# Modulation weights of a three-branch layer stack: from split products to 4-byte products in four column strips

## The reference, cut to what matters

```python
s_lat = jax.nn.silu(c)
s_ctx = jax.nn.silu(c_ctx)[None, :]
...
sh1, sc1, g1, sh2, sc2, g2 = jnp.split(s_lat @ ada_w[i] + ada_b[i], 6, axis=-1)
csh1, csc1, cg1, csh2, csc2, cg2 = jnp.split(s_ctx @ ada_w[i] + ada_b[i], 6, axis=-1)
```

## Time and profile before

| | |
|---|---|
| median of 3 runs | 2079.94 us (2079.64 to 2085.49) |
| profiled execution: time, span | 2084.67 us, 2082.9 us |
| mean granted TensorE clock | 0.943 |
| TensorE busy | 1849.3 us (89%), 12954 products |
| VectorE, ScalarE, GpSimd busy | 908.4, 959.8, 1317.7 us |
| chunks fetched, chunks split | 448, 447 |
| chain that ended last | issue 32%, TensorE 32%, GpSimd 31% |
| waits of TensorE for GpSimd | 46.3 us, all at modulation products (L774) |

### The profile page before, as it was taken

How to read it: one execution, slowest core, us unless ns; L and a number is a source line. 1 busy time by engine, 2 the same in 40 slices (tenths; PEclk the granted TensorE clock), 3 DMA queues, 4 the chain that set the end, 5 groups by cost and what they waited for, 6 DMA issues and landing times.

```text
span 2082.9 us, 36490 instructions
## 1 busy us (share of the span) xinstructions
PE 1849.3 (89%) x12954; PEld 1706.7 (82%) x12954; DVE 908.4 (44%) x1959; ACT 959.8 (46%) x1399; POOL 1317.7 (63%) x451
## 2 busy tenths in 40 slices
PE   5868998999978777999999965699999988888997
PEld 5867898999978776899999953588888877678997
DVE  3688544323335686554313368321221256443223
ACT  5623546544565434555545653532232343255443
POOL 6754578988886744598989961644444433136885
PEclk9988999999999989999999976899999989898999
DMA  6433355655654523465656651433232323114553
GB/s 216 164 127 103 112 176 187 209 196 190 203 184 147 177 91 101 144 210 190 209 186 205 203 188 51 139 101 98 92 101 89 101 76 101 38 64 140 178 189 109
DMA packets 67873, 301.31 MB, mean 145 GB/s; under 512 B 7424, under 2 KB 9728, under 8 KB 67584
## 3 DMA queue, kind: packets, MB, share of 16 engines
q1 hardware_dynamic: 66240, 296.69, 43.0%
q10 hardware_dynamic: 1472, 2.43, 0.3%
HBM read 298.04 MB, written 1.05 MB: 144 GB/s over the span
## 4 chain that ended last, share of the span: by engine, by line
issue 32%; PE 32%; POOL 31%; DVE 2%; ACT 1%; DVEq 1%; POOLq 1%; ACTq 0%
POOL wlo L728 31%; PE bank L762 10%; PE bank L766 10%; PE bank L765 10%; PE bank L1069 0%; DVE bank L1986 0%; PE bank L1073 0%; PE bank L1072 0%; PE bank L1108 0%; POOLq L732 0%; DVE split_acts L1519 0%; DVEq L2145 0%; PE bank L1096 0%; ACT bank L1391 0%; PE bank L1088 0%
## 5 line engine op out<-in xcount | busy, mean ns | idle before, releaser
L728 POOL TENSOR_TENSOR wlo<-raw,whi 128x1280 fp32r<-128x1280 f32 x447 | 1317.5, 2964 | 745.6 <-ACT whi L1142 743.9
L762 PE MATMUL bank<-split_acts,whi 128*128 128x256 f32 (+1 forms) x3556 | 1096.0, 308 | 86.9 <-DVE split_acts L1519 50.9
L765 PE MATMUL bank<-split_acts,whi 128*128 128x256 f32 (+1 forms) x3556 | 1081.4, 304 | 0.0
L766 PE MATMUL bank<-split_acts,wlo 128*128 128x256 f32 (+1 forms) x3556 | 1080.5, 304 | 0.0
L762 PEld LDWEIGHTS bank<-split_acts,whi 128*128 128x128 f32 x3556 | 693.6, 195 | 131.2 <-issue 58.5
L1142 ACT ACTIVATE whi<-raw 128x1280 fp32r<-128x1280 f32 x447 | 562.7, 1267 | 402.8 <-PE bank L762 347.0
L765 PEld LDWEIGHTS bank<-split_acts,whi 128*128 128x128 f32 x3556 | 694.7, 195 | 23.0 <-issue 0.2
L766 PEld LDWEIGHTS bank<-split_acts,wlo 128*128 128x128 f32 x3556 | 693.7, 195 | 23.2
L2018 DVE SCALAR_TENSOR_TENSOR acts<-bank,acts 128x256 f32<-128x256 f32 x120 | 54.1, 480 | 223.2 <-PE bank L766 223.2
L774 PE MATMUL bank<-whi,split_acts 128*128 128x256 f32 x384 | 107.8, 313 | 48.6 <-POOL wlo L728 46.3
L2032 DVE TENSOR_SCALAR acts<-bank 128x512 f32<-128x512 f32 (+1 forms) x64 | 35.7, 558 | 203.1 <-PE bank L766 203.1
(11 more groups left out here) (222 smaller groups left out, 1588.3 us busy)
## 6 DMA issues: line engine op xcount, KB each, us to landing
raw<-in_stream SPq DMA_DIRECT2D x448, 640.0 KB, 3.9
acts<-in_x SPq DMA_DIRECT2D x1, 1024.0 KB, 6.6
acts<-in_ctx ACTq DMA_DIRECT2D x1, 1024.0 KB, 6.6
out<-acts SPq DMA_DIRECT2D x8, 128.0 KB, 2.0
acts<-in_const ACTq DMA_DIRECT2D x1, 832.0 KB, 10.0
acts<-in_const SPq DMA_DIRECT2D x1, 772.0 KB, 9.2
acts<-in_p ACTq DMA_DIRECT2D x2, 256.0 KB, 4.2
acts<-in_par SPq DMA_DIRECT2D x1, 86.0 KB, 3.5
```

What stands on the lines that cost most here:

```text
L728: nc.gpsimd.tensor_tensor(wlo[slot][:, :], raw[slot][:, :], whi[slot][:, :].bitcast(F32), ALU.subtract).then_inc(lo_ready, 1)
L762: first = nc.tensor.matmul(out_ap, w_hi, hi_act(k), start=(k == 0), stop=False)
L765: nc.tensor.matmul(out_ap, w_hi, lo_act(k), start=False, stop=False)
L766: last = nc.tensor.matmul(out_ap, w_lo, hi_act(k), start=False, stop=(k == k_tiles - 1))
```

## The change

The weights of the modulation tiles are no longer split. A tile has two chunks of its own in the stream (eight atoms each, of ten that are fetched), and TensorE reads them straight from the raw buffer, with a stationary operand in 4-byte floats: 32 columns of a small `silu_c` that now lies among the 4-byte buffers. A chunk holds four of the eight parts of the contraction; part k of the first chunk goes to strip k of the array's columns and to partitions 32k to 32k+31 of the bank, the second chunk adds to the same strips. VectorE copies all 128 rows, and `turn_rows` contracts over 128 rows with a `pair` matrix of ones in rows 0 and 1 of every 32, which adds the four strips. The drain behind a tile stands where a count at the last product stood.

SP waits for a raw buffer by the kind of the chunk that was in it: `lo_ready` for a split chunk, `ada_used` (counted by TensorE) for an unsplit one. `chunk_plan` gives the order of both kinds; `keep_ahead` now counts raw chunks of both kinds, `RAW_AT[t] + 3`. A layer has 160 chunks, 124 split and 36 not; the second block 148, 124 and 24; in all 468 fetches and 372 splits. The order of a layer, A for an unsplit chunk, a point for a split one:

```diff
@@ -67,7 +67,7 @@
-            "wo": 8, "hg": 8, "hu": 8, "dn": 11, "pg": 8, "pp": 2, "ada": 16, "turn": 0}
+            "wo": 8, "hg": 8, "hu": 8, "dn": 11, "pg": 8, "pp": 2, "ada": 0, "turn": 0}
@@ -146,11 +146,30 @@
-LAYER_CHUNKS = -(-LAYER_ATOMS // (CHUNK_ATOMS * RING)) * RING
-def last_chunk(span):
-    return max(span[1] - 1, 0) // CHUNK_ATOMS
+SPLIT_CHUNKS = -(-LAYER_ATOMS // (CHUNK_ATOMS * RING)) * RING
+ADA_CHUNKS = 2
+ADA_ATOMS = 2 * KT // ADA_CHUNKS
+def chunk_plan(tiles, spans, split_chunks):
+    order, at, splits, adas = [], {}, 0, 0
+    for t in tiles:
+        if t[0] == "ada":
+            order += [("ada", adas + i) for i in range(ADA_CHUNKS)]
+            adas += ADA_CHUNKS
+        while splits * CHUNK_ATOMS < spans.get(t, (0, 0))[1]:
+            order.append(("split", splits))
+            splits += 1
+        at[t] = len(order) - 1
+    return order + [("split", n) for n in range(splits, split_chunks)], at
+ORDER, RAW_AT = chunk_plan(TILES, ATOM_SPAN, SPLIT_CHUNKS)
+RAW_OF = {c: i for i, c in enumerate(ORDER)}
+LAYER_CHUNKS = len(ORDER)
+LAYER_ADA_CHUNKS = LAYER_CHUNKS - SPLIT_CHUNKS
+assert LAYER_CHUNKS % RING == 0
@@ -159,10 +178,8 @@
-B2_ATOMS_ADA = (ADA_TILES - DEPTH * LAYER_ADA) * 2 * KT
-B2_ATOMS = B2_ATOMS_ADA + 16 + 4 * MLP_T * KT + 64 + 32 + 32 + 64
-B2_CHUNKS = -(-B2_ATOMS // (CHUNK_ATOMS * RING)) * RING
-N_CHUNKS = DEPTH * LAYER_CHUNKS + B2_CHUNKS
+B2_ATOMS = 16 + 4 * MLP_T * KT + 64 + 32 + 32 + 64
+B2_SPLITS = -(-B2_ATOMS // CHUNK_ATOMS)
@@ -208,7 +225,15 @@
+ORDER2, RAW_AT2 = chunk_plan(TILES2, ATOM_SPAN2, B2_SPLITS)
+RAW_OF2 = {c: i for i, c in enumerate(ORDER2)}
...
+FIRST_SPLIT2 = DEPTH * SPLIT_CHUNKS
+FIRST_ADA2 = DEPTH * LAYER_ADA_CHUNKS
+N_CHUNKS = FIRST_CHUNK2 + len(ORDER2)
+EARLY = sum(i < AHEAD for c, i in RAW_OF.items() if c[0] == "split")
+assert EARLY == sum(i < AHEAD for c, i in RAW_OF2.items() if c[0] == "split") == 0
+assert all(RAW_OF[("ada", i)] == RAW_OF2[("ada", i)] == i for i in range(RING))
@@ -300,9 +325,10 @@
-def modulation_atoms(a, n):
+def modulation_atoms(a, m):
+    n, part = divmod(m, ADA_CHUNKS)
...
-    return wide_columns(a["ada_w_2"][layer][:, n * 256:(n + 1) * 256], KT, 256)
+    return wide_columns(a["ada_w_2"][layer][:, n * 256:(n + 1) * 256], KT, 256)[part * ADA_ATOMS:(part + 1) * ADA_ATOMS]
@@ -503,6 +528,7 @@
+        silu_c = keep(2 * KT + 30)
@@ -707,12 +733,24 @@
-            with sp.Fori(1, N_CHUNKS // RING) as r:
-                for slot in range(RING):
-                    sp.wait_ge(lo_ready, r * RING + (slot - RING + 1))
-                    sp.dma_start(raw[slot][:, :], stream[bass.ds(r * RING + slot, 1)].rearrange("a p n -> (a p) n"))\
-                        .then_inc(raw_in[slot], 16)
+            def raw_free(order, c, splits_before, adas_before):
+                kind, n = order[c]
+                if kind == "split":
+                    sp.wait_ge(lo_ready, splits_before + (n + 1))
+                else:
+                    sp.wait_ge(ada_used, adas_before + (n + 1))
+            with sp.Fori(0, DEPTH) as lay:
+                for c in range(LAYER_CHUNKS):
+                    raw_free(ORDER, c, lay * SPLIT_CHUNKS, lay * LAYER_ADA_CHUNKS)
+                    sp.dma_start(raw[c % RING][:, :],
+                                 stream[bass.ds(lay * LAYER_CHUNKS + (c + RING), 1)].rearrange("a p n -> (a p) n"))\
+                        .then_inc(raw_in[c % RING], 16)
+            for c in range(len(ORDER2) - RING):
+                raw_free(ORDER2, c, FIRST_SPLIT2, FIRST_ADA2)
+                fetch(c % RING, FIRST_CHUNK2 + c + RING)
@@ -722,18 +760,18 @@
-            def lo_parts(slot, chunk):
-                pool.wait_ge(hi_ready, chunk + 1)
-                nc.gpsimd.tensor_tensor(wlo[slot][:, :], raw[slot][:, :], whi[slot][:, :].bitcast(F32),
+            def lo_parts(order, n, hi_count):
+                slot, source = n % RING, order[("split", n)] % RING
+                pool.wait_ge(hi_ready, hi_count)
+                nc.gpsimd.tensor_tensor(wlo[slot][:, :], raw[source][:, :], whi[slot][:, :].bitcast(F32),
...
-            used = DEPTH * LAYER_CHUNKS + -(-B2_ATOMS // CHUNK_ATOMS)
-            with pool.Fori(0, used // RING) as r:
-                for slot in range(RING):
-                    lo_parts(slot, r * RING + slot)
-            for slot in range(used % RING):
-                lo_parts(slot, used - used % RING + slot)
+            with pool.Fori(0, DEPTH) as lay:
+                for n in range(SPLIT_CHUNKS):
+                    lo_parts(RAW_OF, n, lay * SPLIT_CHUNKS + (n + 1))
+            for n in range(B2_SPLITS):
+                lo_parts(RAW_OF2, n, FIRST_SPLIT2 + n + 1)
@@ -766,20 +805,23 @@
-            def modulation(b, lay, base):
-                for k in range(KT):
-                    w_hi, w_lo, opens = weights(lay, base, 2)
-                    s4 = silu_c[:, k * P:(k + 1) * P]
-                    first = nc.tensor.matmul(b[:, 0:256], s4, w_hi, start=(k == 0), stop=False)
-                    if opens:
-                        first.then_inc(slots_used, 1)
-                    last = nc.tensor.matmul(b[:, 0:256], s4, w_lo, start=False, stop=(k == KT - 1))
+            def modulation(b, order, chunks_before):
+                for part in range(ADA_CHUNKS):
+                    c = order[("ada", Cursor.ada)]
+                    Cursor.ada += 1
+                    pe.wait_ge(raw_in[c % RING], chunks_before * (16 // RING) + (c // RING + 1) * 16)
+                    for strip in range(4):
+                        k = part * 4 + strip
+                        last = nc.tensor.matmul(b[32 * strip:32 * strip + 32, 0:256], silu_c[:, 2 * k:2 * k + 32],
+                                                raw[c % RING][:, strip * 256:(strip + 1) * 256],
+                                                start=(part == 0), stop=(part == ADA_CHUNKS - 1))
+                    last.then_inc(ada_used, 1)
...
-                    last = nc.tensor.matmul(b[:, 2 * i:2 * i + 2], rows[0:4, i * P:(i + 1) * P], C("pair")[0:4, :],
+                    last = nc.tensor.matmul(b[:, 2 * i:2 * i + 2], rows[:, i * P:(i + 1) * P], C("pair"),
@@ -789,10 +831,10 @@
-                Cursor.atom = 0
+                Cursor.atom = Cursor.ada = 0
...
-                    return lay * LAYER_CHUNKS + chunk
+                    return lay * SPLIT_CHUNKS + chunk
@@ -824,7 +866,8 @@
-                        modulation(b, lay, base).then_inc(gemm_done, 1)
+                        modulation(b, RAW_OF, lay * LAYER_CHUNKS)
+                        pe.drain().then_inc(gemm_done, 1)
@@ -1006,7 +1049,8 @@
-                    last = modulation(b, 0, base2)
+                    modulation(b, RAW_OF2, FIRST_CHUNK2)
+                    last = pe.drain()
@@ -1133,18 +1177,11 @@
-            def split(lay, base, chunk):
-                g = base(lay, chunk)
-                act.wait_ge(slots_used, g + 1)
-                act.wait_ge(raw_in[chunk % RING], (base(lay, chunk - chunk % RING) // RING) * 16 + 16
-                            if isinstance(g, int) else lay * (LAYER_CHUNKS // RING * 16) + (chunk // RING + 1) * 16)
-                sc.activation(whi[chunk % RING][:, :], raw[chunk % RING][:, :], ACT.Copy).then_inc(hi_ready, 1)
-            def ahead(lay, base, chunk):
-                while Split.chunk <= chunk + AHEAD:
-                    split(lay, base, Split.chunk)
-                    Split.chunk += 1
+            def split(n, source, splits_before, chunks_before):
+                act.wait_ge(slots_used, splits_before + (n + 1))
+                act.wait_ge(raw_in[source % RING], chunks_before * (16 // RING) + (source // RING + 1) * 16)
+                sc.activation(whi[n % RING][:, :], raw[source % RING][:, :], ACT.Copy).then_inc(hi_ready, 1)
@@ -1152,23 +1189,18 @@
-            act.wait_ge(silu_act, 2)
-            s4 = silu_c.rearrange("p (k n) -> p k n", n=P)
-            sc.activation(s4[:, :, 0:2], svec[:, 16:32].rearrange("p (k s) -> p k s", s=2), ACT.Copy)\
-                .then_inc(silu_act, 1)
-            for chunk in range(AHEAD):
-                split(0, lambda lay, c: c, chunk)
...
-                Split.chunk = AHEAD
-                def base(lay, chunk):
-                    return lay * LAYER_CHUNKS + chunk
+                Split.chunk = 0
+                def keep_ahead(t, margin=AHEAD):
+                    while Split.chunk < SPLIT_CHUNKS and RAW_OF[("split", Split.chunk)] <= RAW_AT[t] + margin:
+                        split(Split.chunk, RAW_OF[("split", Split.chunk)], lay * SPLIT_CHUNKS, lay * LAYER_CHUNKS)
+                        Split.chunk += 1
...
-                    ahead(lay, base, last_chunk(ATOM_SPAN[t]))
+                    keep_ahead(t)
@@ -1179,8 +1211,8 @@
-                        if name == "mix" and k in (2, 5):
-                            keep_ahead(("ada", k // 3))
+                        if name == "mix" and k == 5:
+                            keep_ahead(("ada", 0))
@@ -1347,18 +1376,16 @@
```

(38 more changed lines are left out.)

28 lines of the change are left out of this document (11 added, 17 removed).

## The result

The changed kernel takes 2088.00 us (median of 13 runs, 2083.79 to 2094.08) where the kernel before takes 2080.99 (13 runs, 2079.64 to 2085.49): a ratio of 1.0032, 95% interval 1.0024 to 1.0040. The forecast of 2067 has the wrong sign; the range of 2044 to 2095 holds the result. In one execution of a kernel further down (the second of the last table) the granted clock was 0.81 and the time 2125.4 us; it is left out of that kernel's ratio.

The account below looks back on a forecast made before the run. TensorE was taken as the bound in most feed-forward and second-block MLP parts, elsewhere waiting for ScalarE's and VectorE's chains or GpSimd's splits. Terms -7.2 - 2.9 - 8.0 - 3.4 + 20.8 - 2.8 - 9.0 = -12.5 gave 2067 us, range 2044 to 2095.

Parts of the forecast that it names:

- Strips: Modulation product on TensorE: four column strips overlap, a tile takes 1.47 us, 0.45 less; -7.2 us over 16 dense tiles.
- MID's waits for GpSimd: TensorE's waits for GpSimd at MID's modulation tiles go: 2.1 us in layer 0, 0.8 in layer 1; -2.9.
- Start: Kernel start: ScalarE begins the first norm earlier, since the first modulation tiles read raw chunks; -8.0 us (bounds -4 and -10).
- Second layer's opening: Norm at the second layer's opening: one single split stays of two pairs on ScalarE; -3.4 us with the waits.
- The norms: Both feed-forward norms: four raw chunks fill the ring, TensorE stands still about 5.5 us, then half clock; +20.8 over two layers.
- Head: Head of each layer: kv reciprocal +2.6 us from ScalarE's waits, against 4 of VectorE's relief; -1.4 a layer, -2.8.
- Second block: Second block: first sum 3.5 us earlier, ada 42 to 47 gain 5.5; -9.0 us (bounds 0 and -14).
- Strips in series: Rival, slower: the four strips run one after the other; +39 us, 2106; chance 0.06.
- Supply: Rival, slower: dense tiles stall at ordinary chunk openings, too few chunks split ahead; +24 us at 1.5 us delay, 2091; chance 0.16.
- Relief: Rival, faster: the ring's stall at the norms is partly hidden, MID's waits for L1520 and slow clock end; 2049; chance 0.20.

Follow-up runs that it names:

- the second of the last table: Changed kernel with rows of four broken up at both norms only, roots ahead of splits, late loads first, second block's adas moved: 2037.66 us, ratio 0.9797.
- loads_first: Changed kernel with SP waiting, behind the second layer's last fetch, for the second block's two late loads before fetching on: 2081.67 us, ratio 0.9991.
- the last set: Four kernels combining the edits on the changed kernel, differing in ada 2's place and the second block's adas: medians 2037.46, 2037.66, 2040.58 and 2036.48 us.

## Why the prediction was wrong

Point by point, in its own numbering.

1. **Strips: right.** From the end of the product before the ada at 318.18 (its start 317.97 + 0.12) to 319.52 is 1.43 us; forecast 1.47. In FFN an ada alone brings the next tile 0.49 us forward, of which 0.09 is given back behind its first product: 0.40 where 0.45 was put. An ada with its turn ahead saves 0.77, which the forecast, with nothing for the turns, did not have: 2.4 us a layer in FFN for 1.8. In one strip the records took 3.64 us, and the next tile began 3.88 after the first of them; the bound had been 3.9.
2. **MID's waits for GpSimd: half right.** Up to the first wo tile, layer 0's MID came out 3.7 us earlier (forecast 3.9), layer 1's not at all (2.6). The wo tiles gave back 1.0 us in each.
3. **Start: right.** The sum enters at 20.87 for 29.48 (forecast "near 21.5"): -8.6, and -9.3 at the second u tile, for -8.0. **But its gain was taken as kept.** That is the first failed step: the stretch from u to kr was costed at nothing, and the -8.0 went into the sum whole. By the second gl tile 1.3 us of the 9.3 are gone. Then 3.0 went to the convolution (9.7 for 6.7), since the splits that used to run under the norm now run beside VectorE. TensorE's stop grew from 2.8 to 5.9 us, and behind it the first products lie 0.21 apart up to 67.92, then 0.12: the 1.2 GHz level and then the full one, 1.5 us more over the 48 products (7.4 for 5.9).
4. **Second layer's opening: right in kind**, -4.8 for -3.4.
5. **The norms: right in place, cause and size** (+4.7 and +6.4 for +4.9 and +5.5). At the ffn norm even the parts agree: the first hg tile comes 3.3 us later (forecast 3.2), and 1.4 more are lost behind it at the lower clock (1.7). The waits of 5.5 and 4.8 us at 368 and 577 are the ones forecast for "about 371 and 572". What the text did not see is how much stood behind it: against a plan without rows of four the same places cost 8.3 and 8.2 us each, 35 us in all with the hole ahead of wo.
6. **Head: the second failed step, by size.** The mechanism stands in the text (ScalarE waits ahead of both roots for chunks behind the four), but the price was read off the reciprocal for kv, +2.6. The root for q, nearer to the four, cost more; setting it free gave 4.1 and 5.1 us. The relief of VectorE that was set against it is there (5.8 us from kn to qr in layer 0, 4 were let go), yet the head as a whole gave +3.7 and +2.3 for -1.4. With the convolution this is 8.8 us of the miss.
7. **Second block: the third failed step**, -3.3 for -9.0. The first sum moved as forecast. But the fetches, which were said to "cost nothing themselves", were priced by the stream's own mean share of the DMA engines. It left out that two single loads run beside it: they landed in 13.1 and 15.5 us for 6.6 and 10.0, and VectorE waited 6.2 for them. With the loads let through first, this part gives about -10. At the last six tiles the chunks land one by one, which the text had; from the first pool tile on the gain was 2.6 us, not 5.5.

The three together are 8.8 + 5.7 of the 19.4 us between -12.5 and +6.9. A further 7.0 lie in layer 1's attention and MID (+4.4 for -2.6), and no run was made to settle them. But *loads_first* (the second block's experiment) has the same two layers, and in its profiled execution the same two stages of layer 1 gave +3.8 (head) and -0.3, where the changed kernel's gave +2.3 and +4.4. So 3.2 us are the spread between two executions, and more may be: two kernels of the last set with the same two layers differ by 5.6 us up to the same ple tile. VectorE's L1668 was waited for 13.0 us in all, its counterpart 9.0 before; it was not tried. The clock was priced behind the two norms alone; part of the losses above is its work elsewhere, and no run takes it apart.

Of the rivals, *Strips in series* was excluded and priced (+49, not +39). *Supply* was not what happened: in the dense window, 400 to 560 us, TensorE is busy 159.2 of 160, for 160.0 before. It is the nearest in time only. *Relief*, no stall at the norms, did not occur, but it is what the rows broken up show as possible.

## What to carry to other kernels

When one ring feeds two kinds of consumer, lay out the order of its slots so that no kind fills the whole ring: otherwise the next fetch of the other kind hangs on a consumer that may itself be waiting. A saving of 221 us on an engine beside the critical path can come out as a loss; look first at what is queued in order behind each wait (here a root behind a split behind a fetch), and at single loads that share the DMA engines with a stream that may now run faster. Price an early start only after you have read the next engine that must keep up with it.

## What the runs showed of the hardware

A VectorE instruction with its inputs in SBUF that meets a GpSimd split took as much as 2.7 us more, whatever its own size: 128x4 elements 2.19 and 2.58 us for 0.17, 128x256 up to 3.17 for 0.48, 128x1024 3.96 for 1.23. Delaying the splits did not lower the sum here, it moved it. Two single loads of 1024 and 832 KB landed in 13.1 and 15.5 us beside the stream and in 7.0 and 8.3 with the stream held; beside it the DMA share was 1.03, at 409 GB/s. Column strips scaled well: 16 records of 256 columns took 1.07 us in four strips and 3.64 in one, 3.4 times. The prediction's estimate from the Trainium skill's 2.38 for three tiles (TensorE: Matmul & The Clock Gate, Measured speedup vs the span model) would have made it 1.11 us for the array part, nearer to the 1.07 of one tile's records than its own 0.88; the whole tile still came out at 1.43, since the switching takes 0.36 us where 0.59 was put.
